# Gate building of a PEER layer: sixteen dense U blocks multiplied ahead instead of eight, their low parts subtracted on GpSimd instead of VectorE

## What is computed

```python
def peer_ffn(x, wq, k1, k2, u, v):          # 1024 tokens, D = 1024, 8 heads, top 16 each
    ...
    expert = jnp.take_along_axis(cand_i, top_pos, axis=-1)      # 128 experts for each token
    gate = jax.nn.softmax(top_s, axis=-1)
    def expert_block(args):
        xb, eb, gb = args
        h = jnp.einsum('td,ted->te', xb.astype(f32), u[eb].astype(f32))
        a = jax.nn.gelu(h, approximate=False) * gb
        return jnp.einsum('te,ted->td', a, v[eb].astype(f32))
```

## Time and profile before

| | us |
|---|---|
| median of 3 runs | 3253.53 (3252.69 to 3258.23) |
| the profiled execution | 3256.87 |
| its span, first to last instruction | 3255.2 |
| gate building, about 1129 to 1513 | 384 |
| `experts`, from about 1514 on | 1741 |

### The profile page before, as it was taken

The page is one execution under the profiler, slowest core; times in us unless marked ns, Lnnn a source line. Parts: engine busy times, 40 slices in busy tenths (PEclk is TensorE's granted clock), DMA queues, the critical chain, the costliest instruction groups (busy, mean ns, idle before and its releaser), DMA issues.

```text
span 3255.2 us, 40544 instructions
## 1 busy us (share of the span) xinstructions
PE 2668.9 (82%) x14888; PEld 2079.1 (64%) x14888; DVE 2411.1 (74%) x5075; ACT 952.6 (29%) x1327; POOL 1637.7 (50%) x1196
## 2 busy tenths in 40 slices
PE   7996688868888366663676999999999999998886
PEld 6886567757666255552444777676667766767774
DVE  4511666644999899994677777787877877779999
ACT  4311433322444334442111222222222222222222
POOL 0001011012777655553666674666665777755674
PEclk9988799989888677886788999999999999999998
DMA  4223322122110279887999998999999999998995
GB/s 133 90 85 98 101 82 69 55 78 83 56 50 21 86 255 310 294 292 279 408 390 384 393 384 329 387 389 396 385 387 338 404 409 406 394 391 298 339 341 180
DMA packets 309933, 833.93 MB, mean 256 GB/s; under 512 B 26128, under 2 KB 114640, under 8 KB 309744
## 3 DMA queue, kind: packets, MB, share of 16 engines
q0 software_dynamic: 150864, 548.60, 44.1%
q1 hardware_dynamic: 158880, 282.83, 24.8%
HBM read 772.45 MB, written 58.88 MB: 255 GB/s over the span
## 4 chain that ended last, share of the span: by engine, by line
DVE 14%; DMA 13%; POOL 10%; PE 9%; issue 6%; ACT 0%; POOLq 0%; DVEq 0%; ACTq 0%
DMA e_u_row<-in_u,id_u 13%; POOL hold L1827 7%; DVE e_u_row L2046 4%; POOL e_u_row L1818 3%; DVE e_y L2036 3%; PE psum L1888 2%; PE psum L1889 1%; PE psum L1890 1%; DVE e_ul L2002 1%; PE psum L1867 1%; PE psum L1869 1%; PE psum L1868 1%; DVE e_vl L2006 1%; DVE hold L2055 1%; DVE e_al L2023 1%
## 5 line engine op out<-in xcount | busy, mean ns | idle before, releaser
L2046 DVE CUSTOM_DVE_ANT_0 e_u_row<-e_u_row,hold 128x1024 f32<-128x1024 f32 x384 | 467.6, 1223 | 275.1 <-DMA e_u_row<-in_u,id_u 240.4
L1818 POOL DMA_INDIRECT e_u_row<-in_u,id_u x384 | 484.1, 1261 | 352.9 <-DVE hidden_s L2046 231.9
L1888 PE MATMUL psum<-e_vh,e_ah 128*128 128x512 f32 x1024 | 427.4, 417 | 144.2 <-DVE e_y L2036 109.9
L1827 POOL DMA_INDIRECT hold<-in_v,id_v x384 | 439.4, 1144 | 141.6 <-issue 113.1
L1889 PE MATMUL psum<-e_vl,e_ah 128*128 128x512 f32 x1024 | 414.2, 405 | 0.0
L1890 PE MATMUL psum<-e_vh,e_al 128*128 128x512 f32 x1024 | 412.3, 403 | 0.0
L1888 PEld LDWEIGHTS psum<-e_vh,e_ah 128*128 128x128 f32 x1024 | 201.0, 196 | 256.5 <-DVE e_y L2036 144.8
L1867 PE MATMUL psum<-x1d_hi,e_uh 128*128 128x512 f32 x864 | 341.0, 395 | 0.0
L1868 PE MATMUL psum<-x1d_lo,e_uh 128*128 128x512 f32 x864 | 337.2, 390 | 0.0
L2036 DVE TENSOR_TENSOR e_y<-e_y,psum 128x512 f32<-128x512 f32 x504 | 323.7, 679 | 18.1 <-PE psum L1890 16.8
L1869 PE MATMUL psum<-x1d_hi,e_ul 128*128 128x512 f32 x864 | 336.3, 389 | 0.0
(11 more groups left out here) (332 smaller groups left out, 5625.2 us busy)
## 6 DMA issues: line engine op xcount, KB each, us to landing
e_vr<-in_v SPq DMA_DIRECT2D x128, 512.0 KB
e_ur<-in_uT SPq DMA_DIRECT2D x108, 512.0 KB
s_G<-g_tile SPq DMA_DIRECT2D x8, 4096.0 KB, 26.3
e_g<-s_G SPq DMA_DIRECT2D x64, 512.0 KB
p_wr<-in_w_ch SPq DMA_DIRECT2D x17, 512.0 KB, 3.9
s_ch<-p_out POOLq DMA_DIRECT2D x16, 512.0 KB, 4.1
m_ch<-s_ch SPq DMA_DIRECT2D x8, 1024.0 KB, 5.9
r_w<-in_wq SPq DMA_DIRECT2D x16, 512.0 KB
```

The lines of the kernel that those rows point to most:

```text
L1818: pool.indirect_dma_start(out=u_ring[n % U_RING][:], out_offset=None, in_=io["u"], in_offset=bass.IndirectOffsetOnAxis(ap=id_u[:, s, k:k + ...
L1827: pool.indirect_dma_start(out=v_ring[m % V_RING], out_offset=None, in_=io["v"], in_offset=bass.IndirectOffsetOnAxis(ap=id_v[:, t:t + 1], a ...
L1888: nc.tensor.matmul(acc, ah[s][j][:, r], vh[s][j][:, c], start=(j == 0), stop=False)
L2046: nc.vector.tensor_tensor_reduce(row, row, xs[:, s, :], 1.0, 0.0, ALU.mult, ALU.add, hs[:, s, k:k + 1]).then_inc(dotted, 1)
```

## The change

`AHEAD_G` becomes 16, so 28 blocks are done ahead instead of 20 and `SHORT` becomes 14: groups 10 to 13 of `experts` load stored hidden values. In `build_gates` a dense block now spans two steps: PE does 12 dense matmuls a step. The low part of the dense block leaves DVE; POOL computes it, ahead of every eighth gather. ACT activates and splits once every two steps. SP stores hidden blocks apart from `G`: `G` after every second one.

```diff
-AHEAD_G = TD // TG
+AHEAD_G = 2 * TD // TG
@@ tensor
-                    b, part = divmod(q, PER)
+                    b, part = divmod(q, PER // 2)
                     if part == 0:
                         pe.wait_ge(u_hi, b + 1)
                         pe.wait_ge(u_lo, b + 1)
...
-                    for k in range(part * KC // PER, (part + 1) * KC // PER):
+                    for k in range(part * KC // 2, (part + 1) * KC // 2):
...
-                    if part == PER - 1:
+                    if part == 1:
                         last.then_inc(h_mm, 1)
@@ vector
-                    if q % PER == 0:
-                        split_u(q // PER)
@@ gpsimd
                 for k in range(P):
+                    if k % (P // AHEAD_G) == 0:
+                        b = k // (P // AHEAD_G)
+                        pool.wait_ge(u_hi, b + 1)
+                        nc.gpsimd.tensor_tensor(ul[:], ur[:], uh[:].bitcast(F32), ALU.subtract).then_inc(u_lo, 1)
                     if k >= U_RING:
                         pool.wait_ge(dotted, k - U_RING + 1)
                     pool.indirect_dma_start(out=ring[k % U_RING], out_offset=None, in_=io["u"],
@@ scalar
+                def split_u(b):
                     act.wait_ge(u_in, 16 * (b + 1))
                     act.wait_ge(h_mm, b)
                     nc.scalar.activation(uh[:], ur[:], ACT.Copy).then_inc(u_hi, 1)
...
+                        if r % 2 == 1:
+                            activate(q // 2)
+                            if q // 2 + 1 < AHEAD_G:
+                                split_u(q // 2 + 1)
@@ sync
-                for b in range(TD // TG):
+                for b in range(AHEAD_G):
                     sp.wait_ge(u_lo, b)
                     sp.dma_start(ur[:], io["uT"][AHEAD_R + b]).then_inc(u_in, 16)
                     if b:
-                        store(sp, b - 1)
+                        store_hidden(sp, b - 1)
+                    if b and b % 2 == 0:
+                        store(sp, b // 2 - 1)
```

More of the change, by code:

```diff
@@ L1596, in _ @@
             def _(dve):
-                def split_u(b):
-                    dve.wait_ge(u_hi, b + 1)
-                    nc.vector.tensor_tensor(ul[:], ur[:], uh[:].bitcast(F32), ALU.subtract).then_inc(u_lo, 1)
                 def dot_rows(k0, k1):
@@ L1641, in _, with activate @@
                     nc.scalar.activation(uh[:], ur[:], ACT.Copy).then_inc(u_hi, 1)
+                def activate(b):
+                    act.wait_ge(h_mm, b + 1)
+                    act.wait_ge(h_out[b % 2], 16 * (b // 2))
+                    nc.scalar.activation(act_out[b % 2][:], psum[:, 6 + b % 2, :], ACT.Gelu).then_inc(gelu, 1)
+                split_u(0)
+                for b in range(TD // TG):
                     act.wait_ge(stored[b % 2], 16 * (b // 2))
@@ L1649, in _ @@
                                                  ACT.Copy).then_inc(evac[n], 1)
-                    act.wait_ge(h_mm, b + 1)
-                    act.wait_ge(h_out[b % 2], 16 * (b // 2))
-                    nc.scalar.activation(act_out[b % 2][:], psum[:, 6 + b % 2, :], ACT.Gelu).then_inc(gelu, 1)
+                        if r % 2 == 1:
+                            activate(q // 2)
+                            if q // 2 + 1 < AHEAD_G:
+                                split_u(q // 2 + 1)
             def store(sp, b):
@@ L1657, in store, with store_hidden @@
                              gt[b % 2].rearrange("p (g j) t -> p g (j t)", j=2)).then_inc(stored[b % 2], 16)
+            def store_hidden(sp, b):
                 sp.wait_ge(gelu, b + 1)
@@ L1667, in _ @@
                     if b:
-                        store(sp, b - 1)
+                        store_hidden(sp, b - 1)
+                    if b and b % 2 == 0:
+                        store(sp, b // 2 - 1)
+                store_hidden(sp, AHEAD_G - 1)
                 store(sp, TD // TG - 1)
@@ L1671, in _ @@
                     sp.wait_ge(stored[n], 16 * (TD // TG // 2))
-                    sp.wait_ge(h_out[n], 16 * (TD // TG // 2))
+                    sp.wait_ge(h_out[n], 16 * (AHEAD_G // 2))
 def spread(first, last, count, slots):
```

## The result

The changed kernel is **slower by 5.8%**: 3443.25 us (3439.42 to 3454.94, four runs) against 3254.16 us, a ratio of 1.0581 with a 95% interval of 1.0566 to 1.0596. The prediction was 3429 us, in a range of 3397 to 3466. The profiled execution took 3454.94 us, the longest of the four; its span of 3453.2 us is 198.0 us above the span before.

A forecast was written before the change was run, and what follows sets the result against it. DVE sets the pace of gate building by busy time, but a closed chain of 34.0 us a block would bound the changed kernel. Stage +180, last stage -4: +176 on the median 3253.53 gives 3429 us, range 3397 to 3466.

The forecast's parts named there:

- The chain: Gate building: a closed loop of waits through DVE, PE, ACT and POOL, once a block: 34.0 us, where two steps took 22.9.
- Link 6: Gap between two POOL instructions, 0.3 us, then gather to its dot: 5.8 us, or 8.2 beside a store of `G`; mean 6.9.
- link 3: PE in step 2b + 1: one-hots 3.7 us, mostly at the high clock, then 12 dense matmuls 3.0; 6.7 us taken.
- longer rival: Gate building: low clock +1.5 us, slower gathers +1.3, slower subtraction +1 per chain; 57 us more, 3486; chance 0.07.
- one-hots of over 5 us: Sign in the profile after: PE's one-hots in a block's second step taking this long would mean the clock was misread.
- The stage: Gate building: first dot later, then fifteen chains, PE done at 1675.6 against 1497.1; 180 us longer in all.
- The last stage: `experts`: groups 10 to 13 load hidden values and gain 0.9 us each, 4 us; bounds 0 and 8.
- the wait is covered: Rival: POOL's 134.5 us of waiting for DVE hold the subtractions; DVE saves 9 us, the last stage 4; 3240; chance 0.03.
- the 8 us that the prediction gave as a sign: Sign in gate building: POOL's subtraction would wait about this long for ACT's high part, sixteen times.
- The port rule: A two-SBUF-input DVE instruction and a GpSimd one reading SBUF share a read port; costs nothing in the chain, where DVE idles.
- 3278: Rival: wait covered, but each of 16 subtractions holds a DVE instruction for 2.38 us, 38 us on 3240; chance 0.02.
- the late load of `g_ur`: SP reaches the next load 18.8 us after a store of `G`; next high part due some 34 us after it, so not late.

The follow-up runs named there:

- e8_warm: The changed kernel with 8 extra matmuls on PE behind the dense part of each block's first step, into a free bank: 3428.7 us, ratio 1.0529.
- e2_pool8: The kernel before, still with eight blocks, only its low parts moved from DVE to POOL, ahead of every sixteenth gather: 3348.4 us, ratio 1.0282.
- e3_late6: The changed kernel with POOL's wait and subtraction in front of gather 8b + 6 instead of 8b: 3279.3 us, ratio 1.0076.
- e7_dve16_sp: The changed kernel with low parts back on DVE, sixteen blocks kept, and the store of `G` one block later on SP: 3262.6 us, ratio 1.0025.
- the edit on SP: Store of `G` issued one block later, behind the load of `g_ur`; with sixteen blocks and low parts on DVE, 3306.5 us without it, 3262.6 with.

## Why the prediction was right

**The chain** (its list of six links). Measured in the profiled execution, link by link, in the mean of the fifteen:

| link | predicted | measured |
|---|---|---|
| 1 dot 8b to PE's one-hots | 5.1 | 5.2 (4.8 to 6.0) |
| 2 one DVE step | 10.9 | 11.1 (10.9 to 12.1) |
| 3 one-hots and 12 dense matmuls | 6.7 | 7.9 (6.6 to 9.5; 8.2 in the turn shown) |
| 4 Gelu and high part | 1.6 | 1.6 |
| 5 POOL's subtraction | 2.45 | 2.4 |
| 6 gap, and gather to dot | 0.3 + 6.9 | 0.1 + 6.84 |
| sum | 34.0 | 35.2 |

Link 6 came out as worked out, in part by luck: the seven gathers beside a store of `G` took 8.4 to 9.1 us to their dot, 8.6 in the mean where 8.2 was put in, and the eight others 4.3 to 6.4, 5.3 in the mean where 5.8 was put in. The two errors cancel. From dot 8b to dot 8b + 8 it was 32.9 to 35.7 us without a store and 35.3 to 37.5 with one; 34 and 36 were predicted.

**The term that was mis-sized is link 3.** I had reasoned that a pause of 1.5 us would leave PE at the high level. In the turn shown the pause was 2.03 us, and the clock fell within the step:

```profile
1377.00:1378.00 1.00, 1.00 (x8) 1.00 (x9) 1.00 (x3) 0.00 (x0) 0.00 (x0) 0.87 0.00 0
1378.00:1379.00 1.00, 1.00 (x7) 1.00 (x7) 1.00 (x3) 0.64 (x1) 0.00 (x0) 0.50 0.00 0
```

From one microsecond to the next the granted clock goes from 0.87 to 0.50, the level of 1.2 GHz, and the one-hots of this step took 5.20 us. Of the 15 second steps that stand ahead of another block, 12 had one-hots of 5.1 to 6.5 us and three of 3.6, as predicted for all; the mean is 4.9. The prediction had this as a part of its longer rival (+1.5 us a chain), and by its own sign, one-hots of over 5 us, I misread the clock. `e8_warm` shows that the pause matters: with most of it filled, the level held in all fifteen. Its length alone does not decide: the three steps that stayed high in the changed kernel came behind 2.96, 1.86 and 1.79 us of pause, while steps behind 1.87 and 2.03 us fell. What else it takes stays open.

**The stage.** From SP's first issue in it to the first gate load of `experts` it is 584.9 us against 386.3: +198.6, where 180 was predicted. The difference is 15 x 1.2 = 18 us of link 3. The first dot started 6.8 us later in its stage; 7.2 was predicted. **The last stage** gained 5.0 us, 4 was predicted. The remaining 4.4 us of the profiled execution's +198.0 arose ahead of the stage, where the two kernels are alike; the medians differ by 189.

**The rivals.** That the wait is covered fell at once: POOL waited 16 us each time. That is twice the 8 us that the prediction gave as a sign. POOL is free once gather 8b - 1 is out, and in the turn shown that was 16.45 us ahead of the high part; the sum does not use this wait, so nothing in the time hung on it. That the order on POOL and not the added work costs the time was an argument; `e2_pool8`, `e3_late6` and `e7_dve16_sp` show it. The port rule cost nothing in the changed kernel, as forecast, since DVE stood idle: its dots take at most 1297 ns there. But where the wait is covered, it decides the sign: 3278 was named, and 3279 and 3282 were measured, with 35 us on DVE where 38 was put in. The prediction read 1.05 us in `retrieve` as agreeing in size with a wait for the whole of POOL's instruction; it was the wait for the second half of it, as shown under `e3_late6`.

**What I did not see** is the late load of `g_ur`. The prediction found it covered by the long chain, which is right, but did not price it for the rival in which the wait is covered: the edit on SP was worth 44 us once DVE did the low parts (42 when each run is taken against its own base).

## What to carry to other kernels

Idle time on an engine is no room for work if that work waits for something that ends later than what is queued behind it: before moving an instruction, write down what stands behind it on the new engine, who waits for that, and whether the loop closes. A busy engine is not relieved by moving work to one that shares its ports: here a low part cost DVE 1.13 us on DVE itself, and 2.15 to 2.78 us when POOL did it beside DVE, at any of the four places tried where DVE had work. And a cost that is covered by a longer one comes back when the longer one is mended, so mend and look again.

## What the runs showed of the hardware that was not expected

- While POOL subtracted for 2.37 us, a run of 16 one-input instructions on DVE took 2.78 us longer (6.96 against 4.18), more than POOL's instruction lasted, and one of the sixteen had all of it (3.10 us); a two-input one took 2.15 us longer (3.37 against 1.22). One that came when half of POOL's subtraction was over lost 1.05 us.
- Behind a 4 MB store in SP's queue the next 512 KB load came so late that ACT waited up to 8.3 us for it, in a block of some 22 us; issued ahead of the store it cost nothing.
- Eight useless matmuls 0.23 us apart, put into the pause of about 2 us in each block, made the kernel 15 us faster, through the granted clock.
